# A two-block network kernel on one core: first norm joined to the set-up, three thin projections in one tile, idle products at three loops left out, a second weight slab split sooner

## What is computed

```python
hn = rms_norm(x, norm_mix_g)
u = hn @ w_in                        # columns: mla 672, fox 1544, ssm 2576, gates 3072
# mla: 0:384 c_q, 384:640 c_kv, 640:672 k_rope
# fox: 672: q, k, v of 512 each, then 8 columns f_raw (2208:2216)
# ssm: 2216: z 1024, xBC 1536, then 16 columns dt_raw (4776:4792)
q = rope(rms_norm(rms_norm(c_q) @ w_uq)); k, v from rms_norm(c_kv) @ w_ukv and k_rope
y_a = softmax(mask(q k^T)) v         # 8 heads, chunk mask
F = cumsum(log_sigmoid(f_raw + b_f)) # y_b: softmax(q k^T + F_i - F_j), causal
dt = softplus(dt_raw + dt_bias)      # y_c: a state space scan over z, xBC, dt
x = x + merged @ w_out
x = x + (silu(gate) * val) @ w_down  # gate, val = conv3(rms_norm(x) @ w_up)
```

## Time and profile before

| what | value |
| --- | --- |
| median of three runs | 2173.28 us |
| the profiled execution | 2174.47 us |
| its span | 2172.7 us |
| PE busy | 2092.5 us, 96% |
| DVE busy | 1138.9 us, 52% |
| ACT busy | 807.0 us, 37% |
| mean granted clock of TensorE | 0.988 |

### The profile page before, as it was taken

How to read it: one execution, slowest core, us unless ns; L and a number is a source line. 1 busy time by engine, 2 the same in 40 slices (tenths; PEclk the granted TensorE clock), 3 DMA queues, 4 the chain that set the end, 5 groups by cost and what they waited for, 6 DMA issues and landing times.

```text
span 2172.7 us, 24120 instructions
## 1 busy us (share of the span) xinstructions
PE 2092.5 (96%) x9821; PEld 1723.2 (79%) x9821; DVE 1138.9 (52%) x1696; ACT 807.0 (37%) x1130; POOL 27.9 (1%) x54
## 2 busy tenths in 40 slices
PE   5999999999999999999999999999999999999986
PEld 4888788888888788888778777788888788888874
DVE  3774555666634566356458776444344444234245
ACT  3645563344422433223232444452323333133132
POOL 0000000010000000000000000000000000000000
PEclk9999999999999999999999999999999999999998
DMA  3321013311333233332233112222222232222231
GB/s 114 98 68 40 20 40 97 95 61 59 98 115 97 78 97 97 97 97 88 87 116 97 59 49 78 85 84 96 98 96 95 88 97 93 96 93 91 97 103 58
DMA packets 164443, 185.52 MB, mean 85 GB/s; under 512 B 4711, under 2 KB 125798, under 8 KB 164334
## 3 DMA queue, kind: packets, MB, share of 16 engines
q1 hardware_dynamic: 160520, 174.96, 25.3%
q10 hardware_dynamic: 3110, 6.90, 0.9%
q0 software_dynamic: 704, 2.13, 0.3%
HBM read 181.86 MB, written 2.12 MB: 85 GB/s over the span
## 4 chain that ended last, share of the span: by engine, by line
PE 92%; DVE 4%; ACT 3%; issue 1%; ACTq 0%; DMA 0%; DVEq 0%
PE ps L383 27%; PE ps L385 27%; PE ps L384 27%; PE ps L476 3%; PE ps L496 2%; PE ps L487 1%; ACT arena L1142 1%; DVE WL L1612 1%; PE ps L653 1%; PE ps L681 1%; PE ps L378 1%; PE ps L458 1%; DVE X L2117 0%; ACT WH L1113 0%; DVE arena L1702 0%
## 5 line engine op out<-in xcount | busy, mean ns | idle before, releaser
L1612 DVE TENSOR_TENSOR WL<-W,WH 128x2048 fp32r<-128x2048 f32 (+2 forms) x168 | 377.8, 2250 | 389.2 <-ACT WH L1113 381.2
L383 PE MATMUL ps<-HH,WH 128*128 128x512 f32 x1416 | 556.0, 393 | 8.6 <-DVE HL L1635 7.3
L384 PE MATMUL ps<-HL,WH 128*128 128x512 f32 x1416 | 552.5, 390 | 0.0
L385 PE MATMUL ps<-HH,WL 128*128 128x512 f32 x1416 | 552.5, 390 | 0.0
L1113 ACT ACTIVATE WH<-W 128x2048 fp32r<-128x2048 f32 (+2 forms) x168 | 315.1, 1877 | 283.6 <-DMA W<-in_w_ff_dram 116.9
L383 PEld LDWEIGHTS ps<-HH,WH 128*128 128x128 f32 x1416 | 266.7, 188 | 67.0 <-issue 7.0
L385 PEld LDWEIGHTS ps<-HH,WL 128*128 128x128 f32 x1416 | 266.7, 188 | 55.9
L384 PEld LDWEIGHTS ps<-HL,WH 128*128 128x128 f32 x1416 | 266.5, 188 | 55.2 <-issue 0.7
L383 PE MATMUL ps<-WH,arena_r 128*128 128x512 f32 (+1 forms) x616 | 240.8, 391 | 6.3 <-DVE WL L1612 3.5
L385 PE MATMUL ps<-WH,arena_r 128*128 128x512 f32 (+1 forms) x616 | 240.1, 390 | 0.0
L384 PE MATMUL ps<-WL,arena_r 128*128 128x512 f32 (+1 forms) x616 | 239.9, 389 | 0.0
(11 more groups left out here) (330 smaller groups left out, 2341.1 us busy)
## 6 DMA issues: line engine op xcount, KB each, us to landing
W<-in_w_in_dram SPq DMA_DIRECT2D x51, 1024.0 KB, 5.2
W<-in_w_ff_dram SPq DMA_DIRECT2D x32, 1024.0 KB, 5.3
W<-in_ffn_w_up_dram SPq DMA_DIRECT2D x44, 512.0 KB, 4.7
W<-in_w_gate_dram SPq DMA_DIRECT2D x16, 1024.0 KB, 5.1
W<-in_ffn_w_down_dram SPq DMA_DIRECT2D x10, 1024.0 KB, 5.0
W<-in_w_out_dram SPq DMA_DIRECT2D x8, 1024.0 KB, 5.0
W<-in_w_branch_dram SPq DMA_DIRECT2D x8, 1024.0 KB, 5.1
W<-in_w_br_ssm_dram SPq DMA_DIRECT2D x4, 1024.0 KB, 5.1
```

The source lines that it names most:

```text
L383: pe.matmul(out_, st[0], mv[0], start=first, stop=False)
L384: pe.matmul(out_, st[0], mv[1], start=False, stop=False)
L385: return pe.matmul(out_, st[1], mv[0], start=False, stop=last)
L1612: dve.tensor_tensor(WL[:, j % RING, 0:n], W[:, j % RING, 0:n], plain(WH[:, j % RING, 0:n]), ALU.subtract).then_inc(slab_lo, 1)
```

## The change

- The stages init and norm1 become one, without the boundary between them. The end of it now splits ahead like that of the others.
- The nine DMAs with the first parameters are issued by SP, ahead of the slabs, not by ACT behind X.
- Before HH and HL only slab 0 is split. The table of relative positions is made between the second and third tile of the norm.
- The third c slab takes three pieces: 160 columns (the last of c_kv, and k_rope), 64 from f_raw on, 32 from dt_raw on. c5 holds k_rope on partitions 0 to 31, f_raw from 32, dt_raw from 96. The slabs fsm and dtsm are gone.
- The other parameters are turned after c1, and `dve_tables` and ACT's Exp and Sin stand after c1 as well.
- The 16 idle products before each loop's first score are gone; the 4 are kept.
- The slabs of fq are split earlier by ACT and DVE, a slab of z at the 17th score of mla, and in the last up tile of each up stage a second slab ahead after its first half.

```diff
-KEEP = {"scores": 16, "weights": 4, "mix": 8, "state": 8, "chunk": 8}
+KEEP = {"weights": 4}
...
                         if s == 0:
-                            keep_clock(b, KEEP["scores"])
...
                     gemm_f("c", w, KT, 0, 2, hn, 2 * i)
                     slab_read()
-                w = slab(KT, 256, win(512, 768))
+                    if i == 0:
+                        pe.wait_ge(params_in, 16 * (len(place) - len(first_params)))
+                        for j in range(1, NPAR):
+                            b = bank(("par", j))
+                            pe.transpose(b[:, 0:P], rows[:, j, :], ident[:, :]).then_inc(pe_done, 1)
+                w = slab(KT, 256, win(512, 672), win(2208, 2272), win(4776, 4808))
...
-                w = slab(KT, P, win(2208, 2208 + P))
-                gemm_f("fsm", w, KT, 0, 1, hn)
-                slab_read()
...
-                w = slab(KT, P, win(4776, 4776 + P))
-                gemm_f("dtsm", w, KT, 0, 1, hn)
-                slab_read()
...
-                "init": pe_init, "norm1": lambda: norm("n1", 0), "mla": pe_mla, "fox": pe_fox,
+                "init": lambda: (pe_init(), norm("n1", 0)), "mla": pe_mla, "fox": pe_fox,
...
+            sp.wait_ge(rows_zero, 1)
+            for ap, start, n in first_params:
+                sp.dma_start(rows[start % P:start % P + n, start // P, 0:ap.shape[1]], ap)\
+                    .then_inc(first_params_in, 16)
             for i, (kt, cols, pieces) in enumerate(slabs):
...
# ACT
-                    split(1)
+                    split(0)
...
+                    if i == 1:
+                        split(slab_of["c", 2])
+                        act.wait_ge(cos_arg, 1)
+                        act.activation(hb[0:SH, 5:6], hb[0:SH, 2:3], ACT.Exp)
+                        act.activation(cosin[:, :, :, :], cosin[:, :, :, :], ACT.Sin).then_inc(cos_done, 1)
                 b = result(("c", 5))
-                freed(act.activation(at(1024, S)[0:ROPE, :], b[0:ROPE, :], ACT.Copy), ("c", 5))
+                freed(act.activation(at(1024, S)[0:96 + SH, :], b[0:96 + SH, :], ACT.Copy), ("c", 5))
...
                 ins.then_inc(head_squares, 1)
+                split(slab_of["fq", 0, 0])
                 root(stat2[:, 0:32])
...
-                b = result(("fsm", 0))
...
+                link(act.activation(v, at(1024, S)[32:32 + HEADS, :], ACT.Identity, bias=hb[32:32 + HEADS, 3:4],
+                                    scale=-1.0))
+                softplus(v, a)
...
-
-                attention("mla", 0, at(2048, 4, S), at(4096, 3, S), at(0, 4, S))
+                use(act, "FT")
+                act.activation(at(6144, S)[0:SH, :], at(1024, S)[96:96 + SH, :], ACT.Identity, bias=hb[96:96 + SH, 1:2],
+                               scale=1.0).then_inc(dt_ready, 1)
+
+                def beside_scores(s):
+                    if s == 16:
+                        split(slab_of["z", 0, 0] - 1)
+                attention("mla", 0, at(2048, 4, S), at(4096, 3, S), at(0, 4, S), beside_scores)
...
# act_ffn1, and the same in dve_ffn1
                             freed(act.activation(raw[:, i % 2, c, 2:2 + S], b[:, :], ACT.Copy), (("up", i), c))
+                            if i == i1 - 1 and c == 0:
+                                split(slab_of[("up", i), c] + 2)
...
# DVE
                 if tag is None:
-                    dve_rel_table()
                     taken(dve, ("par", 0))
                     for t in range(NT):
+                        if t == 2:
+                            dve_rel_table()
                         scaled(t, n, at(XN, NT, DM)[:, t, :]).then_inc(xn_ready, 1)
-                    split(1)
+                    split(0)
...
+                    if i == 1:
+                        split(slab_of["c", 2])
+                        dve_tables()
                 split(slab_of["kr"] + 1)
```

59 lines of the change are left out of this document (23 added, 36 removed).

## The result

The changed kernel takes 2155.36 us (median of six runs, five of them at 2153.23 to 2156.51); the kernel before, timed beside it, 2181.66. The sixth took 2194.67, as some runs of several kernels here do (three of them were profiled, with the clock at half for 89 to 99 us from about 1200 on, and are read only ahead of that); medians include such runs, ratios leave them out. The ratio is 0.9884 with a 95% interval of [0.9855, 0.9914]. So it is faster, as forecast, but 2155 lies over the forecast of 2141 and over its range (2132 to 2153). The profiled execution took 2153.35 us, span 2151.4.

A forecast was written before the change was run, and what follows sets the result against it. The prediction took TensorE as the bound (busy 96% of the span, 92% of the chain); edits of -33.0 and +1.0 for the clock gave -32, from 2174.5 to 2142.5 profiled, median 2141; range 2132 to 2153.

The forecast's parts named there:

- c4's new wait: Fifth c tile: PE waits 2.1 for DVE's low part, behind the moved tables; at least 0, at most 4.
- fsm and fq: Ahead of fk: dropping slab fsm and splitting earlier gives -6.4, of which 0.2 is lost at fq.
- the idle products of mla: Ahead of mla's first score: removal gives -3.63, about 1.1 given back in the loop, so -2.5.
- dtsm and fox: Ahead of fox's first score: dropping slab dtsm and the idle products gives -7.6, the rest covering DVE's evictions of K.
- the band: Ahead of the band's first score: idle products gone, 3.63 less a 0.8 wait for ACT's last V copy, -2.85.
- down1b: Second slab of down1b, split sooner: the 3.47 wait and the half clock behind it go, -5.6.
- I put their landing at 7: Set-up: first parameters land at 7 (5.5 to 9), no wait for their copy; first product at 19.3, -10.8.
- +1.0 as a mean: Half-clock stretches behind new PE pauses (c4, first fox score), each maybe 1.8: +1.0 in all.
- the base: Starting time: profiled execution 2174.5 with span 2172.7, median of the runs 2173.28, 1.2 under the profiled one.
- the loops on a low clock: Rival 1: without idle products the three loops run at low clock, up to 2212 to 2284; chance 0.03.
- Rival 2: Set-up: parameters or slab 0 late, -5 instead of -10.8, total 2147; chance 0.14.
- Rivals 3 and 4: 3: moved waits bite harder, 2147 to 2150, chance 0.15. 4: c4 doesn't wait, clock holds, 2137, chance 0.10.

The follow-up runs named there:

- idle_back: Changed kernel with the 16 idle products back ahead of the first score of the three loops; 2159.12 us.
- best_no_z: Changed kernel with par_late's edit, third c slab split before the tables, scan_mixed_a's order, eight idle products ahead of fox, three ahead of kr; 2135.43 us, ratio 0.979.
- par_late: Changed kernel, but DVE copies the turned parameters between the second and third tile of the norm, not ahead of the first; 2151.24 us.
- scan_later: Changed kernel with eight idle products once ahead of the first product of the scan; 2153.03 us.
- scan_later12: Changed kernel with twelve idle products once ahead of the scan; 2153.33 us.
- b_split_sooner: Kernel before, with a second slab split after the first half of the last up tile of each up stage; 2176.86 us, ratio 0.997.
- z_two: Changed kernel with z's two slabs split apart in the mla loop, at the 9th and the 21st score; 2166.25 us.
- scan_mixed_a: Changed kernel with each scan chunk's rows of decays 2 and 3 issued between the halves of the following gate slab; 2143.52 us, ratio 0.9837.
- scan_fill: Changed kernel with four idle full-width products inside each of the scan's eight thin stretches; 2148.70 us.
- starts_fill: Changed kernel with par_late's edit, third c slab split before the tables, z's first slab split at mla's 17th score, and scan_fill's idle products; 2152.20 us.

## Why the prediction was wrong

**Right.** Each edit behind the set-up, by size and by place: c4's new wait (2.04 for 2.1), fsm and fq (the waits at fk and at K's turning unchanged), the idle products of mla (-3.63 + 1.13 by idle_back, -2.5 as forecast), dtsm and fox (-8.1 for -7.6, with a fall that was before's), the band (-2.8 for -2.85), down1b (-5.1 in the table, 6.1 with the norm's falls taken out, for 5.6). The forecast's sum of edits was -33.0. At the same mean clock the runs of the two kernels differ by 27 (0.989) to 30 (0.983).

**Wrong, first step: "I put their landing at 7".** I had the last parameter issued by 4.7 and landed 2.3 later. The first parameters landed at 10.8 in the profile of the result and at 9.2 to 9.9 in the others with all nine on SP, always 4.7 to 5.4 after the last issue, so my upper end, 9, was too low as well. Why it takes that long stays open; X's last tile isn't what they wait for (best_no_z). The consequence was named too small: I had "+1.3 if the parameters land at 9" for a copy that delays a root, but in DVE's program it stood ahead of all four tiles, and moving it gained 2.3 to 2.8 (par_late, first product at 17.80, ahead of the forecast 19.3). The stretch gave -8.4 for -10.8; of the 2.4 missed, 1.2 goes with the late issue in this one execution, since the second profile has 20.61.

**Wrong, second step: "+1.0 as a mean" for the clock.** The edits' sum of -33.0 stands against -21.3, and 8.7 of these 11.7 lie in unedited stretches: 6.6 in the scan, 1.7 and 1.6 at two norms, less 1.3 at the end, with 1.0 more within n3's row (a fall of 6.83 for one of 3.41). I charged the clock only to pauses that the change makes. There the 1.0 was not far off: c4's wait has a fall behind it in five profiles of twelve. The scan has no pause at all, and I read nothing in it, because nothing in it was edited. But it had falls in the trace of before too, as its 0.98 says. The changed kernel, which comes to the scan 22 us sooner, met six falls where there had been two. That the moment does this and not the edits is shown by the twelve unedited scans and the places of their falls, by scan_later and scan_later12, and by b_split_sooner, which differs from before only beyond 1040 and met four. That the difference was 6.6 against me in this pair of profiles was chance, and by the same chance it could have been nothing (z_two).

**Wrong, third step: the base.** The forecast stood on a profiled execution of 2174.47 with clock 0.988 and on three runs of median 2173.28. All later sets of the kernel before have medians of 2178.6 to 2181.7, at 0.985. From 2180.7 the same sum gives 2148.7; the two sets of the changed kernel gave 2155.36 and 2150.65. So the base is about 7 of the 14 by which the median missed. It can't be added to the second step: the lower medians go with a higher mean clock, so both are falls, once seen in the runs and once in the profiles. The profile of before had two falls in the scan, that of the same code in b_split_sooner four.

Of the rivals, 1 (the loops on a low clock) didn't happen in the changed kernel, whose loops run at 1.00, but the clock fell in the fox loop of ten others without idle products ahead of it (for 6.83 in eight, 3.3 each, for 3.41 in two, 1.6 each), and in none of the seven with some (before and b_split_sooner among them). I gave the idle products' removal no such price. At fox it gains 1.80 (idle_back), and over the 13 profiles without them it costs 2.3 on the mean, so there it paid only where the moment was kind; that the idle products keep these falls away, seven profiles against thirteen suggest, but no pair with all else at the same moment shows it. Rival 2 (the set-up gives half) held in direction: -8.4, or -9.6 in the second profile, lies between the forecast and its -5. Rivals 3 and 4 are out.

The Trainium skill (TensorE: Matmul & The Clock Gate, "HAM oscillation — how this bites in real kernels") tells of pauses between groups that bring the clock down. z_two's 2.95 agrees, and so does c4's wait in five profiles of twelve; in the other seven its 2.04 brought no fall. In the scan the trace shows falls without any pause (PE busy 143.60 of 143.60), which that section doesn't speak of.

**Open.** Why moving one thin stretch out of each chunk also cleared stretches that were left whole (scan_mixed_a), and whether its gain holds wherever the scan comes: six kernels with it had 0 to 2 falls, the twelve executions without it 2 to 8. What sets the moment at the start of an execution wasn't tried.

## What to carry to other kernels

Before forecasting, read the granted clock stretch by stretch over the whole program, also where nothing is edited: a stretch with thin products at 0.98, like this scan, can be at 0.91 after a shift of a few us, and each fall costs half its length. Take the base from many runs with their clocks, not from the profiled one, and compare kernels at equal clock or by stretches. Where thin work has to stand in a row, issue part of a large product within it; that was worth 7.4 us here against the changed kernel's six falls, nearly as much as the largest edits of the change; against before's two falls it would have been 0.7. A copy that nobody needs yet doesn't belong ahead of a chain, and the two halves of a split don't belong in the same step of a loop that lives on that engine.

## What the runs showed of the hardware

- The clock falls to half while PE is never idle: 20 us of 143.6 in the scan, in stretches of 3.41 us that begin at the end of some 4 to 5 us of products of 64 and 128 columns and of 16 rows. With four full-width products in each thin stretch it stayed at 1.00, in two executions (scan_fill, starts_fill).
- In the same code a wait of 2.04 is followed by a fall or not (changed kernel and idle_back). Most falls last 3.41 or 6.83; behind the pause of 2.95 in the mla loop the clock stayed down for 10.24 or 20.5.
- The runs of one kernel lie on its mean clock: 0.983 to 0.989 is 10.4 us of 2150.
- Nine small DMAs issued on SP beside a 2 MB load on ACT's queue landed 4.7 to 5.4 us after the last of them was issued, in 17 profiles, and up to 0.9 after that load's last tile or 0.7 before it.
